# The opening of a two-block transformer kernel: other order of its loads, sums and squares

## The reference, cut to what matters

```
shift, scale, gate = split(silu(c) @ ada_w[0, 0] + ada_b[0, 0], 3)      # c: 1024 numbers; ada_w[0, 0]: 1024 x 3072
h = x * rsqrt(mean(x * x) + 1e-6) * norm_w[0, 0] * (1 + scale) + shift  # x: 256 x 1024
proj = h @ w_in                                                         # then the mixer, and so on
bias = rel_bias[bucket of the distance]                                 # added to the windowed scores
```

## Time and profile before

| | us |
|---|---|
| median of 3 runs (lowest, highest) | 970.56 (968.07, 971.42) |
| the profiled execution, its device time | 968.6 |
| its span in the profile | 966.9 |
| TensorE busy | 889.4 (92%) |
| VectorE busy | 702.7 (73%) |
| ScalarE busy | 451.7 (47%) |
| first product of block 0 starts | 49.31 |

### The profile page before, as it was taken

The page is one execution under the profiler, slowest core; times in us unless marked ns, Lnnn a source line. Parts: engine busy times, 40 slices in busy tenths (PEclk is TensorE's granted clock), DMA queues, the critical chain, the costliest instruction groups (busy, mean ns, idle before and its releaser), DMA issues.

```text
span 966.9 us, 17652 instructions
## 1 busy us (share of the span) xinstructions
PE 889.4 (92%) x7016; PEld 853.9 (88%) x7016; DVE 702.7 (73%) x888; ACT 451.7 (47%) x566; POOL 58.0 (6%) x104
## 2 busy tenths in 40 slices
PE   2499979899999997699999999999999999999996
PEld 1288869799999997699999999988989999999996
DVE  5888898788877778766665556865577777776565
ACT  2247453466643333256664433544465444444445
POOL 2110110211111110000000000000000000000000
PEclk9889999899999997689999999999999999999998
DMA  8995765399988886047665555464335655655531
GB/s 323 334 327 180 234 196 171 121 319 321 330 294 298 295 295 207 22 141 229 217 219 186 192 186 174 142 196 131 133 97 185 197 174 174 210 183 161 168 127 44
DMA packets 156600, 196.60 MB, mean 203 GB/s; under 512 B 5341, under 2 KB 143116, under 8 KB 156556
## 3 DMA queue, kind: packets, MB, share of 16 engines
q1 hardware_dynamic: 142732, 145.64, 46.9%
q0 software_dynamic: 13824, 50.34, 14.0%
HBM read 194.90 MB, written 1.06 MB: 203 GB/s over the span
## 4 chain that ended last, share of the span: by engine, by line
PE 74%; DVE 13%; issue 5%; ACT 4%; DMA 2%; SPq 1%; DVEq 0%; ACTq 0%; POOLq 0%
PE G L558 15%; PE G L559 14%; PE G L560 14%; PE A L558 6%; PE A L560 6%; PE A L559 6%; DVE w_lo L1110 3%; ACT w_hi L1761 3%; DMA ada_raw<-in_ada_w_dram 2%; PE G L633 2%; PE G L635 2%; PE G L634 2%; PE A L686 2%; DVE ada_acc L1129 2%; DVE HN L1272 1%
## 5 line engine op out<-in xcount | busy, mean ns | idle before, releaser
L1110 DVE TENSOR_TENSOR w_lo<-raw,w_hi 128x2048 fp32r<-128x2048 f32 x135 | 307.0, 2274 | 172.0 <-ACT w_hi L1761 171.8
L1761 ACT ACTIVATE w_hi<-raw 128x2048 fp32r<-128x2048 f32 x135 | 256.6, 1900 | 271.9 <-PE A L560 138.6
L558 PE MATMUL G<-h_hi,w_hi 128*128 128x256 f32 x880 | 258.8, 294 | 27.0 <-DVE h_lo L1255 14.7
L559 PE MATMUL G<-h_lo,w_hi 128*128 128x256 f32 x880 | 254.4, 289 | 0.0
L560 PE MATMUL G<-h_hi,w_lo 128*128 128x256 f32 x880 | 254.1, 289 | 0.0
L558 PEld LDWEIGHTS G<-h_hi,w_hi 128*128 128x128 f32 x880 | 174.2, 198 | 33.7 <-issue 28.9
L559 PEld LDWEIGHTS G<-h_lo,w_hi 128*128 128x128 f32 x880 | 174.6, 198 | 0.2 <-issue 0.2
L560 PEld LDWEIGHTS G<-h_hi,w_lo 128*128 128x128 f32 x880 | 174.4, 198 | 0.0
L558 PE MATMUL A<-u_hi,w_hi 128*128 128x256 f32 x512 | 143.7, 281 | 5.8 <-DVE X L1233 5.1
L559 PE MATMUL A<-u_lo,w_hi 128*128 128x256 f32 x512 | 143.0, 279 | 0.0
L560 PE MATMUL A<-u_hi,w_lo 128*128 128x256 f32 x512 | 143.0, 279 | 0.0
(11 more groups left out here) (310 smaller groups left out, 1319.9 us busy)
## 6 DMA issues: line engine op xcount, KB each, us to landing
raw<-in_mlp_w_dram SPq DMA_DIRECT2D x64, 1024.0 KB, 5.3
ada_raw<-in_ada_w_dram POOLq DMA_DIRECT2D x88, 512.0 KB, 5.0
raw<-in_w_in_dram SPq DMA_DIRECT2D x14, 1024.0 KB, 5.1
raw<-in_w_up_dram SPq DMA_DIRECT2D x11, 1024.0 KB, 5.3
raw<-in_w_gate_dram SPq DMA_DIRECT2D x11, 1024.0 KB, 5.4
raw<-in_attn_w_in_dram SPq DMA_DIRECT2D x9, 1024.0 KB, 7.5
raw<-in_w_down_dram SPq DMA_DIRECT2D x8, 1024.0 KB, 5.0
raw<-in_attn_w_out_dram SPq DMA_DIRECT2D x4, 1024.0 KB, 4.9
```

What stands on the lines that cost most here:

```text
L558: pe.matmul(dst, wh, ah, start=start, stop=False)
L559: pe.matmul(dst, wh, al, start=False, stop=False)
L1110: dve.tensor_tensor(w_lo[n % 2][:, 0:k, :], raw[n % RAW][:, 0:k, :], w_hi[n % 2][:, 0:k, :].bitcast(F32), ALU.subtract).then_inc(lo_done, 1)
L1761: act.activation(w_hi[n % 2][:, 0:k, :], raw[n % RAW][:, 0:k, :], ACT.Copy).then_inc(hi_done, 1)
```

## The change

- SP loads c second and x third, behind the first constants; the small constants and the 13 other small loads come behind them. c has a semaphore of its own (`c_in`) and is transposed by itself (bank use "c").
- POOL no longer waits, ahead of f3, for the small loads.
- f0 to f7 are now the scale's and f8 to f15 the shift's; before they alternated.
- VectorE starts its sums from the c that comes out of the accumulation memory; it no longer squares X. ScalarE squares each pair of X tiles into a tile of its own, and TensorE adds the four tiles (8 products in place of 2).
- SP issues the load of weight block 0 ahead of the hankel load, and the hankel load waits until ten of the sums are used (f0 to f9).
- TensorE does ms0 and the scale's transposes ahead of the flips, and the shift's behind them; VectorE finishes the scale's part and `split_lo(0)` ahead of f12; ScalarE does `split_hi(0)` and `root(0)` ahead of the copies to BIAS.

The diff, cut to its core:

```diff
 def first_block(t):
-    return ((1, 0)[t % 2], t // 2) if t < 2 * DT else (2, t - 2 * DT)
+    return (1, 0, 2)[t // DT], t % DT
...
 # SP
                 sp.dma_start(C[:, 0:C_DECAY], shape_consts[:, 0:C_DECAY]).then_inc(consts_in, 16)
-                sp.dma_start(C[:, C_DECAY:], shape_consts[:, C_CNT:C_ALL]).then_inc(consts_in, 16)
+                sp.dma_start(vrows[0:DT, 3, :], c[0].rearrange("(t p) -> t p", p=P)).then_inc(c_in, 16)
+                sp.dma_start(x_rows, x[0].rearrange("(k p) d -> p k d", p=P)).then_inc(x_in, 16)
+                sp.dma_start(C[:, C_DECAY:], shape_consts[:, C_CNT:C_ALL]).then_inc(small_in, 16)
...
                 bank_was_read(sp, "table")
                 sp.dma_start(scratch.ap(), t8[:, :]).then_inc(table_out, 16)
+                load(N_ATTN, w_in[:, :, ATTN_COLS[0]:ATTN_COLS[0] + COLS])
                 sp.wait_ge(table_out, 16)
+                sp.wait_ge(ada_used, 10)
                 sp.dma_start(hankel[:, :, :],
...
 # GpSimd
-                if f == 3:
-                    pool.wait_ge(vecs_in, 16 * 14)
...
 # TensorE
+            pe.wait_ge(consts_in, 16)
+            pe.wait_ge(c_in, 16)
+            bank_done("c", pe.transpose(bank_empty(pe, "c")[:, 0:DT], vrows[0:DT, 3, :], C[0:DT, C_ID:C_ID + DT]))
...
+            pe.wait_ge(x_in, 16)
+            turn_x(0)
+            turn_x(1)
+            pe.wait_ge(vecs_in, 16 * 13)
...
+            pe.wait_ge(small_in, 64)
...
+            turn_x(2)
+            turn_x(3)
+            dst = bank_empty(pe, "ms0")
+            for q in range(4):
+                pe.wait_ge(ssq_ready, q + 1)
+                for m in range(2):
+                    last = pe.matmul(dst[:, 0:S], ones[:, :], pool_squares[q][:, m, :],
+                                     start=q == 0 and m == 0, stop=q == 3 and m == 1)
+            bank_done("ms0", last)
+            turn_sums(0, "scale", DT)
             pe.wait_ge(table_in, 16)
             for q in range(4):
                 dst = bank_empty(pe, f"flip{q}")
                 bank_done(f"flip{q}", pe.matmul(halves(dst), anti, hankel[:, 2 * q:2 * q + 2, :],
                                                 start=True, stop=True))
-            mean_square(0)
-            turn_sums(0, "scale", 2 * DT - 1)
             turn_sums(0, "shift", 2 * DT)
...
 # VectorE
+            ada_next(5)
             src = bank_full(dve, "vecs")
-            bank_read("vecs", dve.tensor_copy(V[:, :], src[:, 0:V_ALL]))
+            bank_read("vecs", dve.tensor_copy(V[:, 0:V_C], src[:, 0:V_C]))
             src = bank_full(dve, "table")
             bank_read("table", dve.tensor_copy(t8[:, P:2 * P], src[0:HEADS, 0:P]))
...
-            for t in range(2 * DT):
-                ada_next(1)
-                if t % 2 and 3 <= t < 11:
-                    q = (t - 3) // 2
-                    bank_was_read(dve, f"x{q}")
-                    add_squares(2 * q, q == 0)
+            ada_next(7)
             dve.wait_ge(g_split, 1)
...
+            chain(part(0, "scale"))
+            factor(0)
             split_lo(0)
-            modulation(0)
+            ada_next(4)
+            part(0, "shift").then_inc(mod_ready, 1)
+            dve.wait_ge(mod_ready, 1)
+            ssq[0] = 4
             norm("n0", 0, GAIN[:, 0, :], MOD[:, 0, 0:DT])
...
 # ScalarE
             for q in range(4):
                 src = bank_full(act, f"x{q}")
+                act.activation(pool_squares[q][:, :, :], halves(src), ACT.Square).then_inc(ssq_ready, 1)
                 bank_read(f"x{q}", act.activation(X[:, 2 * q:2 * q + 2, :], halves(src), ACT.Copy))
```

More of the change, by code:

```diff
@@ L341, in take_each @@
                 take(name, bank)
-        take_each(("vecs", 0), ("table", 1), ("x0", 2), ("x1", 3), ("x2", 0), ("x3", 1), ("flip0", 2),
-                  ("flip1", 3), ("flip2", 0), ("flip3", 1), ("ms0", 2), ("scale0a", 3), ("scale0b", 0), ("shift0a", 1),
-                  ("shift0b", 2))
+        take_each(("c", 1), ("vecs", 0), ("table", 1), ("x0", 2), ("x1", 3), ("x2", 0), ("x3", 1),
+                  ("ms0", 2), ("scale0a", 3), ("scale0b", 0), ("flip0", 1), ("flip1", 2), ("flip2", 3), ("flip3", 0),
+                  ("shift0a", 1), ("shift0b", 2))
         S0, T0, V0 = ([f"{name}0{v}" for v in range(ATT_UNITS)] for name in ("scores", "turned", "att_out"))
@@ L719, in attention, with turn_x @@
                     weighted(r, v - 2)
-            pe.wait_ge(consts_in, 32)
-            pe.wait_ge(vecs_in, 16 * 14)
-            dst = bank_empty(pe, "vecs")
-            for slot, count, at in ((0, P, 0), (1, 77, 128), (2, 3 * F2T, V_CONVW), (3, DT, V_C)):
-                last = pe.transpose(dst[:, at:at + count], vrows[0:count, slot, :],
-                                    C[0:count, C_ID:C_ID + count])
-            bank_done("vecs", last)
-            pe.wait_ge(small_in, 48)
-            bank_done("table", pe.matmul(bank_empty(pe, "table")[0:HEADS, 0:P], rb[:, :],
-                                         C[0:32, C_HOT:C_HOT + P], start=True, stop=True))
-            pe.wait_ge(x_in, 16)
-            for q in range(4):
+            pe.wait_ge(consts_in, 16)
+            pe.wait_ge(c_in, 16)
+            bank_done("c", pe.transpose(bank_empty(pe, "c")[:, 0:DT], vrows[0:DT, 3, :], C[0:DT, C_ID:C_ID + DT]))
+            def turn_x(q):
                 dst = bank_empty(pe, f"x{q}")
@@ L739, in _ @@
                 bank_done(f"x{q}", last)
+            pe.wait_ge(x_in, 16)
+            turn_x(0)
+            turn_x(1)
+            pe.wait_ge(vecs_in, 16 * 13)
+            dst = bank_empty(pe, "vecs")
+            for slot, count, at in ((0, P, 0), (1, 77, 128), (2, 3 * F2T, V_CONVW)):
+                last = pe.transpose(dst[:, at:at + count], vrows[0:count, slot, :],
+                                    C[0:count, C_ID:C_ID + count])
+            bank_done("vecs", last)
+            pe.wait_ge(small_in, 64)
+            bank_done("table", pe.matmul(bank_empty(pe, "table")[0:HEADS, 0:P], rb[:, :],
+                                         C[0:32, C_HOT:C_HOT + P], start=True, stop=True))
+            turn_x(2)
[8 more added lines that the diff above has]
+            turn_sums(0, "scale", DT)
             pe.wait_ge(table_in, 16)
@@ L1125, in ada_sum @@
                     return
[L1126 removed]
+                since = 3 if ADA_C <= f < ADA_E else 2 if ADA_B <= f < ADA_C else 1
                 step = 2 if f >= ADA_E else 6
```

28 lines of the change are left out of this document (14 added, 14 removed).

## The result

The changed kernel took 973.63 us (median of 9 runs, 970.04 to 976.37) against 969.58 for the kernel before (9 runs, 967.74 to 971.58): ratio 1.0044, 95% interval 1.0025 to 1.0063. It is slower by 0.2 to 0.6%, where 0.6% faster was forecast. Its profiled execution has a span of 973.9 us against 966.9. These two single executions lie 7.0 us apart and the medians 4.1, so what follows shares out more than the medians' difference.

The account below looks back on a forecast made before the run. The opening, VectorE's sums and their loads, was taken to hold TensorE until block 0 at 49.3 us. f15 used at 38.1 plus a 5.7 tail gave 43.8, saving 5.5 from 970.56: 965.1 us, range 961.2 to 968.9.

Parts of the forecast that it names:

- The small loads 13.3, as before: Opening, SP's queue: the small loads land at 13.3 us as before, so block 0 is issued at about 15.0.
- f11 used at 25.4: Opening, VectorE: f11 lands at 24.1 us and is used by 25.4, against 33.0 before.
- Vanish in the waits: Opening, VectorE: the vecs and table copies among the sums, under 1 us, cost nothing beside the waits for loads.
- The new wait of w_lo, 1.3: Ahead of f12, VectorE's w_lo of block 0 waits 1.3 us for w_hi, as block 0 lands at 26.7.
- rival B: SP's queue starves, block 0 lands near 30 and starts at 47.1: 968.4 us, no change that can be told; chance 0.22.
- f15 used at 38.1: End of the opening's sums: f15's load lands at 36.8 us after 4.45, and VectorE uses it at 38.1.
- The flips under f15 with 0.7 us of cover: TensorE's flips follow a hankel load landing at 31.7 us and end at 37.4, ahead of f15's use, costing nothing.
- rival C: Late hankel load holds flips and shift's transposes: block 0 at 48.8, 970 us; 974 if the load takes 20; chance 0.06.
- The tail, 5.7: From f15's use to block 0's first product: transposes, reductions, addition and norm take 5.7 us, against 8.7 before.
- Nothing here is held by absolute time, so the rest of the chain shifts with block 0: Behind block 0: everything later moves earlier with block 0's start, keeping the whole 5.5 us.
- Rival D: The gain is given back behind block 0 by block 2 landing late: 968 to 970 us; chance 0.07.
- A with an early f11: Block 0 lands in time, no new w_lo wait (963.8 us, chance 0.2); with f11 early too, given as 961.7.

Follow-up runs that it names:

- b_scale_first: The kernel before with only the scale's eight sums and loads put ahead of the shift's eight: 972.04 us against 971.24, ratio 1.0006.
- b_scale_first_dve: `b_scale_first` with VectorE's scale part, factor and w_lo of block 0 ahead of the last four sums: 973.37 us against 970.30, ratio 1.0023.
- b_all4: The kernel before with squares on ScalarE, flips behind the shift's transposes, c first, scale's sums first, block 0 ahead of the hankel load: 970.81 us, ratio 1.0014.

## Why the prediction was wrong

**Silu(c) at 5.5**: 5.0, right. **VectorE becomes the one that waits**: right, and it waited for more than loads.

**"The small loads 13.3, as before"** is the step that failed first. They landed at 20.8. In the order before, 14 small loads went first, with only three modulation loads beside them, and the last four, behind x, still had only those beside them until 11.2; now x and nine modulation loads were issued by 6.2 us, and everything SP issued later stood behind them. I had put x into the sum of bytes, and held the same small loads, which stand behind x in the same queue, to be untouched. The Trainium skill ("DMA: Bandwidth & Descriptors", section "Queues, rings and completion order") says that a DMA engine alternates between its queues packet by packet. The trace agrees: f0 and f1, together as large as x, were there at 11.8 and x at 12.0. I had written down what the rule makes of x and of f1, and not carried it to the loads behind x.

**f11 used at 25.4**: 30.7. f11 landed at 25.7 instead of 24.1, inside my bounds, and by that alone would have been used at 27.0. The rest came from the copies of vectors and table that stand ahead of f5 in VectorE's program. "Vanish in the waits" was wrong by 3.7 us: a copy that is late itself is a wait, and the seven sums behind it take 8.9 us.

**The new wait of w_lo, 1.3**: absent. Block 0's load was issued 7 us later than I took, when of the modulation's loads only f10 and f11 were outstanding, and landed in 6.5; w_hi was ready 2 us before VectorE came to w_lo. My rival B, a starved block 0, did not occur.

**f15 used at 38.1**: 41.5; 3.4 late, as f12 was 3.9 late and f15's load took 3.8 instead of 4.45. **The flips under f15 with 0.7 us of cover**: the duration of the hankel load was right (9.1), its issue was 5.5 us later, so the flips ended at 43.5, 2.1 behind f15. That is rival C's mechanism, at a price that I had worked out (each us later costs one) and given to C alone. That C's first case has block 0 at 48.8 is luck: there the load was slow, here it was issued late. **The tail, 5.7**: 5.15 from the flips' end. Together: 43.8 + 3.4 + 2.1 - 0.6 = 48.7.

**"Nothing here is held by absolute time, so the rest of the chain shifts with block 0"** is the second step that failed, and it alone decides the sign. Between blocks 33 and 46 it gave back 4.4 us, and 4.6 and 5.0 in the two repeats of both programs; the 1.5 us in block 0 were this trace's. Rival D had this idea with another place and 0.07. A slip besides: A with an early f11 is 963.8 - 1.6 = 962.2, not 961.7; it does not touch the outcome.

What the 4.4 us are made of is shown by rows: late loads, sums ahead of the residual, longer gaps of TensorE (1.3), short stretches of low clock behind them (3.1). Taking the sum out of the way took the low clock and more away, but not the loads' lateness. Two things are open: why gaps of the same length were followed by a low clock only in the programs with late loads, and why the loads land a few tenths later in some programs than in others, 250 us behind the edit. It is not the semaphores, x's place, the flips' place, SP's order, c's place or the order of loads, each by itself; the pair `b_scale_first` and `b_scale_first_dve` suggests that VectorE's order can switch it, `b_all4` that something else can too, each by single traces.

## What to carry to other kernels

Moving a load to the front of a queue moves all the others back: follow the last small load of the queue, and each instruction that an engine has behind it, before pricing what the early one brings. Put work that waits for a transfer behind the instruction that releases TensorE, not ahead of it; this one line was worth more than the whole opening. It did not make the kernel insensitive to late loads: 3.4 us still hung on them. And where a gain is forecast at the start of a long kernel, look further back for places with no slack: here a column end waited for each modulation load that came a few tenths late. Take a second trace before sharing out a difference of 1 or 2 us: the opening of one and the same program scattered by 2.8.

## What the hardware showed that I had not expected

- A load of 4 KB took 11.1 us to land behind 1,024 KB on its own queue with nine loads of 512 KB issued on the other; before, behind the same 1,024 KB with three such loads on the other, it took 4.9.
- A gap of TensorE of 1.60 us was followed by full clock in the kernel before (1.00), one of 1.96 at the same place by 3.4 us at 0.50 in the changed kernel; one of 2.05 at the third column end was not. A hit costs 1.55 us, and the gap's length alone does not say whether it comes.
- With the flips right ahead of the norm TensorE had a granted clock of 1.00 through block 0 in all five traces, where it had 0.74 to 0.86 in the other fifteen. The products took 10.1 to 10.4 us of TensorE instead of 11.5 (before) and 12.4 (after).
- VectorE's sums of 128x1024 into one accumulator start 1.39 us apart, into alternating ones 1.20.
